# Gated delta rule of a two-layer trunk: decay rows and diagonal blocks spread by transfers through DRAM, the inverse turned by VectorE, lower matrices prepared two steps ahead

## The reference, cut to what matters

```
g_cum    = cumsum(g)                                 # log decays, within the chunk
decay    = exp(g_cum_i - g_cum_j)  for j <= i, else 0
lower    = beta_i * (k_i . k_j) * decay,  j < i      # strictly lower triangle
u        = inverse(I + lower) @ (beta * (v - decayed k @ S))
out      = (decayed q) @ S + ((q . k) * decay) @ u
S        = S * total decay + (decayed k)^T @ u       # carried to the next chunk
```

## Time and profile before

| | |
|---|---|
| median of three runs | 1874.83 us (1873.88 to 1875.99) |
| the profiled execution's span | 1875.7 us |
| TensorE busy | 1626.5 us, 87% |
| VectorE busy | 830.0 us, 44% |
| ScalarE busy | 467.5 us, 25% |
| GpSimd busy | 280.3 us, 15% |
| delta phase, layer 0 | 389.3 to 601.2 us |
| delta phase, layer 1 | 1281 to 1492 us |

### The profile page before, as it was taken

The page is one execution under the profiler, slowest core; times in us unless marked ns, Lnnn a source line. Parts: engine busy times, 40 slices in busy tenths (PEclk is TensorE's granted clock), DMA queues, the critical chain, the costliest instruction groups (busy, mean ns, idle before and its releaser), DMA issues. The chain is left out here.

```text
span 1875.7 us, 23996 instructions
## 1 busy us (share of the span) xinstructions
PE 1626.5 (87%) x9277; PEld 1016.6 (54%) x9277; DVE 830.0 (44%) x1656; ACT 467.5 (25%) x832; POOL 280.3 (15%) x446
## 2 busy tenths in 40 slices
PE   5899997977997966999679999987799796799993
PEld 3555564545876534454355555654587653455443
DVE  1378323555885241111154970355688524111115
ACT  2211132253231122122131111335423112222221
POOL 0200211014632012000102000001463201200002
PEclk9999998878998987999889999987899898799996
DMA  9621799900001008999591201460000100899974
GB/s 336 137 79 45 209 304 360 382 17 1 2 2 57 2 23 315 366 365 364 215 240 45 90 23 56 152 258 1 1 1 2 57 2 34 317 395 367 365 278 179
DMA packets 114398, 302.31 MB, mean 161 GB/s; under 512 B 28000, under 2 KB 36098, under 8 KB 101250
## 3 DMA queue, kind: packets, MB, share of 16 engines
q1 hardware_dynamic: 66576, 221.18, 31.7%
q0 software_dynamic: 14080, 53.48, 8.3%
q10 hardware_dynamic: 33650, 26.37, 5.1%
HBM read 234.91 MB, written 67.05 MB: 161 GB/s over the span
## 5 line engine op out<-in xcount | busy, mean ns | idle before, releaser
L691 PE MATMUL ps<-hreg,ring 128*128 128x512 f32 x768 | 397.1, 599 | 11.1 <-ACT hreg L1327 11.1
L692 PEld LDWEIGHTS ps<-hreg,ring 128*128 128x128 f32 x768 | 147.1, 192 | 185.3 <-issue 185.3
L1160 PE MATMUL ps<-ring,tok 128*128 128x512 f32 x544 | 238.0, 596 | 0.2 <-issue 0.2
L1160 PEld LDWEIGHTS ps<-ring,tok 128*128 128x128 f32 x544 | 104.1, 192 | 130.6 <-issue 130.6
L692 PE MATMUL ps<-hreg,ring 128*128 128x128 f32 x768 | 148.5, 275 | 0.0
L2172 DVE TENSOR_TENSOR work<-work,ps 128x256 f32<-128x256 f32 x34 | 14.2, 421 | 250.6 <-ACT work L1587 250.6
L1175 PE MATMUL ps<-ring,work 128*128 128x512 f32 x272 | 124.1, 600 | 0.0
L691 PEld LDWEIGHTS ps<-hreg,ring 128*128 128x128 f32 x768 | 117.7, 194 | 11.7 <-issue 11.7
L1724 DVE SCALAR_TENSOR_TENSOR mixA<-cin_reg,small,mixA 128x655 f32<-128x655 f32 x120 | 107.2, 896 | 0.0
L2176 DVE COPY zs<-ps 128x1024 f32<-128x1024 f32 x34 | 41.6, 1225 | 122.5 <-PE ps L1175 122.5
L1738 DVE SCALAR_TENSOR_TENSOR tmp_reg<-mixb_reg,small,tmp_reg 128x642 f32<-128x642 f32 x96 | 84.7, 883 | 0.0
(11 more groups left out here) (357 smaller groups left out, 2773.4 us busy)
## 6 DMA issues: line engine op xcount, KB each, us to landing
ring<-in_w SPq DMA_DIRECT2D x102, 1024.0 KB, 8.3
ring<-in_w_mod SPq DMA_DIRECT2D x24, 2048.0 KB, 12.3
ring<-in_w_in SPq DMA_DIRECT2D x12, 2048.0 KB, 8.4
ys<-zs ACTq DMA_DIRECT2D x34, 512.0 KB, 7.8
tok<-xs SPq DMA_DIRECT2D x30, 512.0 KB, 11.4
xs<-zero POOLq DMA_DIRECT2D x8, 1792.0 KB, 19.8
ys<-zero POOLq DMA_DIRECT2D x8, 1664.0 KB, 20.7
ring<-in_w_out SPq DMA_DIRECT2D x4, 2048.0 KB, 12.7
```

The source lines that it names most:

```text
L691: mm(o[:, 0:TS], lhs(k), rhs(k)[:, 0:TS], start=k == 0, stop=k == nk - 1)
L692: ins = mm(o[:, TS:T], lhs(k), rhs(k)[:, TS:T], start=k == 0, stop=k == nk - 1)
L1160: ins = mm(bank(2 + q), xgT[q][:, k, :], w, start=k == 0, stop=k == KD - 1)
```

## The change

- **Decay rows.** Two matmuls a layer compute g_cum for all tiles in transposed form; ScalarE copies them to SBUF, and its queue stores them to a DRAM tensor `gc_rows`. SP loads them back, the same row on all 128 partitions, into `ring[2]` (two loads of 1 MB for the latent tiles, later two of 256 KB for the context tile). `decay_rows` is gone. `decay_logs` is now a `scalar_tensor_tensor` on two SBUF operands, the row and a mask of 0 and a large negative number, so that `query_mask` is gone too.
- **Diagonal blocks.** `diag_pick` is followed by a store of its 64 KB tile to the DRAM tensor `diag_own`, by SP, and by a load in which 16 partitions read the same 16 rows (1 MB into `ring[0]`). The load of step `j` waits for the inverse of `j - 1`. `diag_spread`, `diag_rows` and `diag_copies` are gone.
- **Inverse.** `inverse_spread` is eight ScalarE copies with a scale for each partition; `inverse_turn` is VectorE's transpose, once for each direction. `turn_inverse` and `inverse_copies` are gone.
- **Two steps ahead.** `lower_mats`, `diag_blocks` and `diag_pick` of `j + 2` stand at the end of step `j` (before: those of `j + 1` in its first third). `gram_kk` of `j + 2` and `gram_kq` of `j + 1` take other places in TensorE's stream.
- **Copies.** The copy of L1980 and the first output copies go from VectorE to ScalarE.
- The second half of w_out is loaded after the last use of `ring[2]` by the rows, during step 3.

The diff, cut to its core:

```diff
+                def rows_load(d, first, n):
+                    src = bass.AP(tensor=gc_rows, offset=((l * 2 + d) * 8 * NCH + 8 * first + 4 * d) * P, ap=[[0, P], [8 * P, n], [1, 4 * P]])
+                    at0 = 2048 * d + (0 if n == 4 or d == 0 else 3 * 512)
+                    sp.dma_start(ring[2][:, at0:at0 + 512 * n].rearrange("p (c n) -> p c n", c=n), src).then_inc(rows_loaded.sem, 16)
+
+                def diag_load(j):
+                    need(dn_rhs, j + 1)
+                    sp.dma_start(diag_own.ap()[l, j], dsm[:, 0:P]).then_inc(aux_stored.sem, 16)
+                    need(aux_stored, 16 * (j + 2))
+                    if j:
+                        need(dn_inv, j)
+                    src = bass.AP(tensor=diag_own, offset=(l * NCH + j) * P * P, ap=[[BASE * P, P // BASE], [0, BASE], [1, BASE * P]])
+                    sp.dma_start(diag, src).then_inc(diag_loaded.sem, 16)
...
-                def decay_rows(j):
...
-                def diag_rows(j, part):
...
-                def turn_inverse(j):
...
                 mm(ps[:, 532:552], cst[:, C_LO:C_LO + P], gsp[:, :, 4:8], start=True, stop=True)
-                mm(ps[:, 552:592], ones, gsp[:, :, :], start=True, stop=True).then_inc(gc_done.sem, 1)
+                mm(ps[:, 552:592], ones, gsp[:, :, :], start=True, stop=True)
+                all_g = gsp.rearrange("p c n -> p (c n)")
+                mm(ps[0:8 * NCH, 1536:1536 + P], all_g, cst[:, C_UP:C_UP + P], start=True, stop=True)
+                mm(ps[0:8 * NCH, 1536 + P:1536 + 2 * P], all_g, cst[:, C_LO:C_LO + P], start=True, stop=True)\
+                    .then_inc(gc_done.sem, 1)
...
+                A_(gcT, ps[0:8 * NCH, 1536:1536 + 2 * P], ACT.Copy)
                 A_(cdec, gcum[:, 40:80], ACT.Exp).then_inc(gc_exp.sem, 1)
+                need(gc_exp, 1)
+                act.dma_start(gc_rows.ap()[l].rearrange("d r t -> r d t"), gcT.rearrange("r (d t) -> r d t", d=2))\
+                    .then_inc(aux_stored.sem, 16)
...
+                def inverse_spread(j):
+                    need(dn_inv, j + 1)
+                    for d in range(2):
+                        for b in range(64 // BASE):
+                            ins = A_(B[d]["XT64"][j % 2][:, :, BASE * b:BASE * b + BASE], dinv[:, d], ACT.Copy,
+                                     scale=cst[:, C_B8 + b:C_B8 + b + 1])
+                        ins.then_inc(dn_xt.sem, 1)
...
                         for h in range(4):
-                            ins = V.tensor_scalar(B[d]["DT"][:, h, :], row_bank(j, d)[:, h * P:(h + 1) * P],
-                                                  col(gcum, d, chunk(j, d), h), 0.0, ALU.subtract, ALU.min)
+                            ins = V.scalar_tensor_tensor(B[d]["DT"][:, h, :], decay_row(j, d)[:, h * P:(h + 1) * P],
+                                                         col(gcum, d, chunk(j, d), h), tri, ALU.subtract, ALU.add)
...
+                def inverse_turn(j):
+                    for d in range(2):
+                        need(dn_xt, 2 * j + d + 1)
+                        V.transpose(B[d]["X"].rearrange("p h n -> p (h n)"), B[d]["XT64"][j % 2].rearrange("p h n -> p (h n)"))\
+                            .then_inc(dn_lv.sem, 1)
```

More of the change, by code:

```diff
@@ L289, in build, with out_first, chunk @@
         B[0]["kdec"], B[1]["kdec"] = half(tmp_reg, 0), half(rst, 0)
-        diag = [ring[0][:, 1024 * d:1024 * d + 1024] for d in range(2)]
-        diag4 = [r.rearrange("p (h k m) -> p h k m", h=4, k=BASE) for r in diag]
+        diag = ring[0][:, 0:BASE * P]
+        def out_first(j, d):
+            return j < 2 or (j == 4 and d == 0)
+        def chunk(j, d):
+            return 4 if j == 4 else (j if d == 0 else 3 - j)
         def qk_tile(t):
@@ L297, in pbank, with decay_row @@
             return bank(6 + d) if j else bank(1 + 2 * d)
-        def row_bank(j, d):
-            return bank(3 * d) if j else bank(1 + 2 * d)
+        def decay_row(j, d):
+            held = j if j < 4 else 0
+            return ring[2][:, 2048 * d + 512 * (held if d == 0 else 3 - held):][:, 0:512]
         dsm = sb("dsm", [P, 640])
@@ L542, in _ @@
                     ring_load(("mod", n))
-                for i in range(2):
-                    ring_load(("out", l, i))
+                ring_load(("out", l, 0))
+                def rows_load(d, first, n):
[10 more added lines that the diff above has]
+                    sp.dma_start(diag, src).then_inc(diag_loaded.sem, 16)
+                slot_free(held_before[("out", l, 1)])
+                need(aux_stored, 16)
+                for d in range(2):
+                    rows_load(d, 0, 4)
+                diag_load(0)
+                need(dn_dlog, 2)
+                need(dn_erow, 2)
+                for d in range(2):
+                    rows_load(d, 4, 1)
+                for j in range(1, NCH):
+                    diag_load(j)
+                need(dn_dlog, 10)
+                need(dn_erow, 10)
+                ring_load(("out", l, 1))
                 def up_load(q, e):
@@ L850, in _ @@
                 need(mod2_ready, 1)
-                def chunk(j, d):
-                    return 4 if j == 4 else (j if d == 0 else 3 - j)
                 def cols(cc):
@@ L875, in gram_kk @@
-                def gram_kk(j):
-                    for d in range(2):
-                        if j:
-                            need(dn_pcopy, 6 * j - 1 + d)
-                        else:
-                            need(dn_dlog, d + 1)
-                            need(dn_erow, d + 1)
-                        for h in range(4):
-                            kk = dnT[:, 4 + h, cols(chunk(j, d))]
-                            ins = mm(pbank(j, d)[:, hcol(h)], kk, kk, start=True, stop=True)
-                        ins.then_inc(dn_prep.sem, 1)
@@ L905, in turn_inverse, with gram_kk @@
[L905 to L912 removed]
+                def gram_kk(j, d):
+                    if j:
+                        need(dn_mat, 4 * j - 1 + d)
+                        need(kv_copied, 8)
+                    else:
+                        need(gc_exp, 1)
+                    for h in range(4):
+                        kk = dnT[:, 4 + h, cols(chunk(j, d))]
+                        ins = mm(pbank(j, d)[:, hcol(h)], kk, kk, start=True, stop=True)
+                    ins.then_inc(dn_prep.sem, 1)
@@ L914, in level_w, with gram_kq @@
+                def gram_kq(j, d):
+                    need(dn_mat, 4 * j + d + 1)
+                    for h in range(4):
+                        c_ = cols(chunk(j, d))
+                        ins = mm(pbank(j, d)[:, hcol(h)], dnT[:, 4 + h, c_], dnT[:, h, c_], start=True, stop=True)
+                    ins.then_inc(dn_prep.sem, 1)
                 def level_w(j, i):
@@ L1018, in _ @@
                     ins.then_inc(kv_turned.sem, 1)
-                    if t == 1:
-                        diag_rows(0, 0)
-                    if t == 3:
-                        diag_rows(0, 1)
                 need(rope_x, 8)
-                gram_kq(0)
-                decay_rows(1)
-                need(kv_copied, 8)
-                turn_inverse(0)
+                for j in range(2):
+                    for d in range(2):
+                        (gram_kk if j else gram_kq)(j, d)
                 for j in range(5):
@@ L1951, in _ @@
                         diag_pick(0)
-                        diag_spread(0)
-                query_mats(0, query_mask(0))
+                for d in range(2):
+                    query_mats(0, d)
                 decay_logs(1)
-                inverse_spread(0)
+                lower_mats(1)
+                diag_pick(1)
+                inverse_turn(0)
                 for j in range(5):
@@ L2289, in diag_inverse @@
                         left, back = BASE - 1 - n, BASE - 1 - n
-                        row = both_ways(ring[0], BASE * n + n + 1, 1024 + BASE * back, BASE * BASE, left)
+                        row = both_ways(ring[0], P * n + n + 1, P * back + 64, BASE, left)
                         have = both_ways(dsm, 128 + n, 192 + back, BASE, left, across=True)
```

232 lines of the change are left out of this document (94 added, 138 removed).

## The result

The changed kernel takes 1920.65 us (median of four runs, 1918.79 to 1921.05) against 1875.12 us: a ratio of 1.0242, 95% interval 1.0222 to 1.0261. It is **slower by 2.4%**, 28 us above the upper end of the range that was given. The profiled execution has a span of 1919.0 us, 43.3 us more than that of before.

A forecast was written before the change was run, and what follows sets the result against it. No engine is full; a 30.9 us chain from mask to mask bounds each delta step. Start +4.3 and steps -1.2, +0.6, +1.9, -3.9, -0.3 give +1.4 a layer, +2.8 for both: 1877.6 us, range 1854 to 1893.

The forecast's parts named there:

- the load of 1 MB: Delta phase, each step's diagonal blocks from DRAM: lands in 7.2 us, carried by eight engines in place of sixteen.
- The upper bound taken: Slowest figure taken for that load: 8.3 us, the median of weight loads when several stand in line.
- the meeting at the port: In the inverse: VectorE's eight decay logs hold up GpSimd by 1.2 us, four times a layer, bounds 0 and 2.2.
- the +1.4 of the forecast: Net change in us of one layer's delta phase: start +4.3, steps -1.2, +0.6, +1.9, -3.9, -0.3.
- The start: Start of the delta phase up to its first mask: +4.3 us, mask at 457.7 against 453.42.
- Rival 2: Inverse: the logs cost GpSimd 2.2 us, not 1.2, each time; 1885.6 us, or 1891.6 with slow spread; chance 0.15.
- Rival 1: Load of the diagonal blocks lands in 4.7 us, by sixteen engines; 1859.4 us in all; chance 0.30.
- Rival 4: Round trip through DRAM: store 2.3 and load 8.3 us, 8.5 us a layer more; 1894.6 us; chance 0.07.
- break-even of 8.6 us: Limit for the DRAM round trip: store and load of 8.6 us, the replaced way of 8.7 less 0.1.
- Rival 3: Inverse and load: the logs cost GpSimd nothing, eight engines carry the load; 1868.0 us; chance 0.08.
- The clock: Sign of being wrong: TensorE's granted clock falls in the steps, as it has less to do; no size given.
- 2.8 us to spare: TensorE's side of a step: 28.7 us, 2.8 under the new loop, so relieving TensorE brings nothing by itself.

The follow-up runs named there:

- e1: Changed kernel, load's source with 16 repeats outside and 8 blocks inside (computes wrong numbers): 1897.74 us, delta phases 207.9 / 208.4 us.
- e11: Changed kernel, load reading 16 groups of 8 different weight-matrix rows (computes wrong numbers): delta phases 211.3 / 211.0 us.
- e3: Changed kernel, 64 KB tile stored twice so the load's source has 16 outer rows, each read 8 times: 1887.94 us, 1.0064 of the kernel before.
- e2: Changed kernel, 1 MB load cut by columns into two 512 KB loads on the same queue: 1908.1 us, 1.0174 of the kernel before.
- e13: Kernel before with only the decay rows coming from DRAM and w_out's second half asked for behind the last logs: 1882.75 us, 1.0026.

## Why the prediction was wrong

**The step that failed** is the load of 1 MB: "I take 7.2, above the nearest row". It took 11.1 to 12.1 us, and 14.8 beside w_out. The half of the argument that came from the source was right: eight engines, which the prediction said no row showed, are in the trace now, as eight closing packets, and e1 shows that they follow the outer count. With the rule of the Trainium skill that the prediction named ("DMA: Bandwidth & Descriptors", section "Why a DMA increments its semaphore by 16 and not by 1") the traces agree: 8 closing packets where the source's outer dimension counts 8, 16 where it counts 16. The half that failed is the packet, priced at 0.33 us from a load whose source is a list (and even that was divided among all 144 packets; the 128 that carry data take 0.37). Eight engines at 0.53 us make 8.5 us of packets where some 5 were counted. The upper bound taken, 8.3 us, was a bound on another kind of load and held nothing: a median of loads that wait in line says nothing on one with half the engines.

**The rest of the sum held, in part by luck.** Loads longer than 7.2 by 4.9, 4.1, 3.9, 3.9 and 7.6 us are 24.4 a layer; the meeting at the port that did not happen takes 4 x 1.2 away; with the +1.4 of the forecast that is +21.0. Measured are +22.4 and +23.1, and the difference is the remainder of two misses that offset each other in part. The steps come out well one by one (forecast, plus load, less meeting; then measured): 32.6 and 32.2, 34.2 and 33.6, 35.5 and 35.8, 35.9 and 35.5; together they are 1.2 us under. The single prices: store 1.56 us (1.7), spread 2.02 (2.0), transpose 0.45 (0.4), corners 2.55, last step 22.0. The start is 2.6 us over: from the first gate matmul to the first mask it is 10.6 us longer than before (64.1, now 74.7), where 4.3 + 4.9 - 1.2 are 8.0. Two terms were too small. From the gates to the first pick there are 2.2 us more (38.1, now 40.3) where 1.0 was counted; that the pick comes at 426.23 all the same, ahead of the forecast 428.4, is because the whole phase begins 3.4 us earlier. And the second pick meets GpSimd, a meeting that the prediction put at nothing:

```profile
456.35 2.48 POOL L2265 TENSOR_TENSOR work<-work,dnT 128x512 f32<-128x512 f32 x2
456.48 1.22 DVE L1901 TENSOR_SCALAR dsm<-dsm,cst 128x128 f32<-128x128 f32 x1 [16.79 <-ACT dsm L1490]
457.74 1.25 DVE L1902 SCALAR_TENSOR_TENSOR dsm<-dsm,cst 128x128 f32<-128x128 f32 x1
```

The two operations take 2.5 us where they take 0.64 elsewhere, 1.8 us on the path to the first mask, and in layer 1 as well (1.22 and 1.25).

**The meeting at the port** (1.2 us for GpSimd, four times a layer) takes place three times, since the late load lets the logs at 435.44 pass before the inverse, and costs GpSimd nothing. The inverse with eight logs in it lasts from 505.50 to 517.54, 12.0 us, as without (499.14 to 511.21). VectorE pays: eight logs take 2.18 us where GpSimd rests and 3.09 inside the inverse (2.77 to 3.28 over both layers),

```profile
435.44 2.18 DVE L1878 SCALAR_TENSOR_TENSOR hreg<-ring,small,cst 128x128 f32<-128x128 f32 x8
```

and there it has time; at the second pick of a layer, above, it has none. Rows 9 had shown this side only, VectorE standing until GpSimd was through; that GpSimd waits as well was my addition. Rival 2 falls with it.

**The rivals.** Rival 1 was not what happened, but its price was right: -7.7 us a layer was forecast against before, and -6.8 to -8.7 measured where the load takes 5.2 to 5.4 us. Two errors help it, loads 0.5 to 0.7 longer than its 4.7 and no meeting. Rival 4 was what happened, at more than twice its price (9.9 us a layer with the forecast's 1.4, measured 22.4 and 23.1): "the round trip hides nothing", with 8.3 for the load. Its break-even of 8.6 us from the store's issue to the inverse is somewhat low: with 9.1 e1 is 3.4 us below the phase of before in layer 0 and e11 level with it, and with 10.2 e3 is 3.0 above. So it lies between 9.1 and 10.2; that the other prices came out lower, the meeting above all, is my reason for it. Rival 3 (no meeting) was right in the meeting and in the eight engines, and wrong in the load's time.

**Chances.** All of them hung on the load, and the range left no room for one slower than 8.3. A price that no row shows should have been bounded from above by the nearest slow thing: half the engines and a packet at twice its time.

**The clock** fell to 0.78 in a step, as the prediction said it might. That it did not decide is argued, by no run of its own: with each step explained to 0.6 us by loop and load, nothing is left for it. It stands on TensorE's side, which had 2.8 us to spare by the forecast and more with the longer load.

## What to carry to other kernels

When work is moved from an engine to a transfer, price the transfer in its own form: count the outermost dimension of its access patterns (a source of 8 used eight engines here, of 16 sixteen), and take the time of a packet from a transfer whose source is grouped in the same way; the same megabyte took 5.2, 7.5 or 11.1 us here by its source alone. An engine that is 87% busy over the program may be free on the loop that sets a phase; write the loop down with its links, and take out a link, not work. And where a slow link can't be made fast, ask which wait puts it in line: putting the pick ahead of an instruction that waits for the inverse was worth 56 us here (with w_out's load put behind it). Its phases, 201.4 and 203.8 us with the slow load, are as short as those with the fastest load in the old order, 202.6 and 200.9.

## What the runs showed of the hardware

- A load whose source has 8 outer rows closes with 8 small packets and uses 8 engines; two such loads behind each other are served one after the other, as by the same 8 (e2: closing packets at 498.7 to 499.0 and at 502.2 to 502.8 us).
- 8 KB packets took 0.33 to 0.35 us with a plain list of 128 rows, 0.53 to 0.58 with grouped sources whether rows repeat or not, and 0.81 to 0.84 where sixteen engines read one row of 8 KB into 16 neighbouring partitions.
- VectorE's operation on two SBUF operands is lengthened by GpSimd's work (from 0.27 to 0.39 us each, eight in a row, beside GpSimd's small operations; the pick from 0.64 to 2.5 us beside two of 128x512). GpSimd's chain of 31 is not lengthened (12.0 us with the logs in it, 12.1 without).
- A store of 64 KB in 8 groups of rows takes some 1 us longer to the next instruction than a plain one (2.56 against 1.56 us, with two such stores side by side).
- TensorE's granted clock in a step does not follow its busy time alone: 1.00 at 28.64 us of records in 31 (before), 0.94 at 27.41 and 1.00 at 26.95 (e13), 0.78 at 24.60 (changed).
